# The norms' inverse root as Ln and Exp on ScalarE, in place of Sqrt there and a reciprocal on VectorE

## The chip, the cores and the metric

The kernel runs on one core of a Trainium2 chip. The metric is the time of one run on the device in microseconds, the median of three runs.

## The reference

Two transformer blocks over 512 tokens of 1024 columns, all in float32. The first block has a gated linear attention (GLA, 4 heads), a state-space layer (S5) and a mixture of 32 experts with 4 per token; the second has a state-space layer, a window attention, a full attention whose query and key heads are normed, and a gated ffn. Around and inside them stand RMS norms, all of one form:

```
def rmsnorm(x, g):
    xf = x.astype(jnp.float32)
    r = lax.rsqrt(jnp.mean(xf * xf, axis=-1, keepdims=True) + EPS)
    return (xf * r * g.astype(jnp.float32)).astype(x.dtype)

h = x
hn = rmsnorm(h, mix_pre_g) * (1 + sc1) + sh1        # first norm
...                                                 # GLA: o = rmsnorm(o, gla_norm_g) for each head; S5
h = h + g1 * rmsnorm(mix, mix_post_g)               # the mixer's post-norm
hn2 = rmsnorm(h, ffn_pre_g) * (1 + sc2) + sh2       # ahead of the router
h = h + g2 * rmsnorm(moe_ffn(hn2), ffn_post_g)      # the experts' post-norm
...                                                 # second block: norms of x and of the context,
...                                                 # of the q and k heads, ahead of the ffn, and the last one
```

## The kernel before

Activations are kept with the features on the 128 partitions and the tokens along the free dimension: a tensor of 1024 x 512 is 8 tiles of 128 x 512. A norm over features is therefore a sum over partitions. ScalarE squares each tile (line 415), TensorE multiplies the squares by a matrix of ones, so that each partition of one PSUM bank gets the sums of all 512 tokens (`pe_norm`), ScalarE takes the square root out of that bank (line 418), VectorE takes the reciprocal in place (line 437) and scales the 8 tiles by gain and inverse root (line 440), and ScalarE adds the shifts (line 424). Matmuls of the next layer wait for the last shifted tile.

There are 18 such norms, 16 over 512 columns and two over 256 (the context's). Their reciprocals stand in five places of VectorE's program: `dve_norm` (line 437, 5 of them), `dve_gla_out` (line 832, one for each of 4 heads), `dve_add_normed` (line 1284, the two post-norms with the addition to the residual), `dve_att_in` (line 2940, 5 heads' tiles of 512 columns and one of 256, in the second attention) and `dve_out` (line 3344). In the two loops over heads the steps share one buffer for the root. In GLA the head's outputs come from 22 matmuls, ScalarE squares and copies them (lines 867 and 869) once VectorE is done with the head before, and TensorE sums. In the second attention ScalarE squares the next head's tile (line 2916) right after the root of this one, and takes the next root when VectorE has scaled this head (line 2943). One more norm, of the state-space layer, has 4 columns with the tokens on the partitions; it keeps Sqrt and reciprocal.

Each engine runs its own program in order, and semaphores join them. `act_done` and `dve_done` are counted by an engine for itself: it waits on its own results before it reads them. ScalarE evaluates a function from the set of tables that is loaded. Where an activation needs a function outside the loaded set, the build puts a set load (ACT_TABLE_LOAD) in front of it. Copy, Square, Identity and Abs are in every set; Sqrt, Sin, Silu, Sigmoid, Gelu and Exp are each in others; one set has both Ln and Exp.

Weights come through six panel buffers (four in the second block) of 2 MB that the SP queue fills as TensorE gives them back. GpSimd loads the router's weights and biases after the mixer's post-norm (`pool_moe_loads`), and casts and subtracts the gate biases when they have landed (`pool_bias`, lines 1404 and 1408); that runs beside the norm ahead of the router.

Of the kernel before, what the change touches and what calls it, by code (L numbers as in the profile page):

```python
# [11 lines left out]
ACT = mybir.ActivationFunctionType  # L12
# [10 lines left out]
GLA_HEADS, DK, DV, CHUNK = 4, 64, 128, 64  # L23
# [12 lines left out]
HD = 64  # L36
# [243 lines left out]
def build(nc, a, table, where, out):  # L280

    ctx = ExitStack()
    with ctx:
# [23 lines left out]
        eps_col = sb("eps_col", [P, 1])  # L307
# [52 lines left out]
        act_done = sem("act_done")  # L360
# [41 lines left out]

        def act_norm(act, step, src, sq, std, n, kt, dim, shifts=None, dst=None, after=None, copied=False):

            for k in range(kt):
                if after is not None:
                    act.wait_ge(after.sem, after.next(act))
                if copied:  # L410
                    act.wait_ge(to_act.full, to_act.next_full())
                    bank = to_act.take()
                    act.activation(src[:, k, :], bank[:, 0:n], ACT.Copy).then_inc(to_act.free, 1)
                    act.wait_ge(to_act.free, to_act.own_reads())
                act.activation(sq[:, k, :], src[:, k, :], ACT.Square).then_inc(sq_ready.sem, 1)  # L415
            act.wait_ge(to_act.full, to_act.next_full())
            bank = to_act.take()
            act.activation(std, bank[:, 0:n], ACT.Sqrt, scale=1.0 / dim, bias=eps_col[:, 0:1]).then_inc(to_act.free, 1)
            act.wait_ge(to_act.free, to_act.own_reads())
            act.sem_inc(std_ready.sem, 1)  # L420
            if shifts is not None:
                for k in range(kt):
                    act.wait_ge(scaled.sem, scaled.next(act))
                    act.activation(dst[:, k, :], dst[:, k, :], ACT.Identity, bias=shifts[k]).then_inc(normed.sem, 1)  # L424
# [9 lines left out]

        def dve_norm(dve, step, src, dst, std, kt, factors):
            dve.wait_ge(std_ready.sem, std_ready.next(dve))
            dve.reciprocal(std, std).then_inc(dve_done, 1)
            dve.wait_ge(dve_done, step.next())
            for k in range(kt):
                dve.scalar_tensor_tensor(dst[:, k, :], src[:, k, :], factors[:, k:k + 1], std,  # L440
                                         ALU.mult, ALU.mult).then_inc(scaled.sem, 1)
# [242 lines left out]
        o_std = alr  # L684
# [144 lines left out]

        def dve_gla_out(dve, step, h):  # L830
            dve.wait_ge(ostd_ready.sem, ostd_ready.next(dve))
            dve.reciprocal(o_std, o_std).then_inc(dve_done, 1)
            dve.wait_ge(dve_done, step.next())
            dve.scalar_tensor_tensor(o_sb, o_sb, col("gla_norm_g"), o_std, ALU.mult, ALU.mult).then_inc(dve_done, 1)
            dve.wait_ge(dve_done, step.next())
            if h == 0:
                dve.wait_ge(gla_act.sem, gla_act.next(dve))
            dve.tensor_tensor(hidden[:, h, :], o_sb, og[:, h, :], ALU.mult).then_inc(dve_done, 1)
            dve.wait_ge(dve_done, step.next())
            dve.sem_inc(gla_out.sem, 1)  # L840

        def act_gla(act, step):
            act_project(act, step)
            act.wait_ge(gla_dve.sem, gla_dve.next(act))
            act.activation(work, bsum, ACT.Abs).then_inc(act_done, 1)
# [12 lines left out]
            act.activation(work, work, ACT.Exp, scale=1.0 / TAU).then_inc(act_done, 1)  # L858
            act.wait_ge(act_done, step.next())
            act.sem_inc(gla_act.sem, 1)  # L860
            act_project_rest(act, step)
            for h in range(GLA_HEADS):
                act.wait_ge(to_act.full, to_act.next_full())
                bank = to_act.take()
                if h >= 1:
                    act.wait_ge(gla_out.sem, gla_out.next(act))
                act.activation(o_sq, bank[:, :], ACT.Square).then_inc(act_done, 1)
                act.wait_ge(act_done, step.next())
                act.activation(o_sb, bank[:, :], ACT.Copy).then_inc(to_act.free, 1)
                act.wait_ge(to_act.free, to_act.own_reads())  # L870
                act.sem_inc(osq_ready.sem, 1)
                act.sem_inc(o_ready.sem, 1)
                act.wait_ge(to_act.full, to_act.next_full())
                bank = to_act.take()
                act.activation(o_std, bank[:, :], ACT.Sqrt, scale=1.0 / DV, bias=eps_col[:, 0:1]).then_inc(to_act.free, 1)
                act.wait_ge(to_act.free, to_act.own_reads())
                act.sem_inc(ostd_ready.sem, 1)


# [401 lines left out]
        def dve_add_normed(dve, step, branch, std, gains):  # L1281

            dve.wait_ge(std_ready.sem, std_ready.next(dve))
            dve.reciprocal(std, std).then_inc(dve_done, 1)
            dve.wait_ge(dve_done, step.next())
            for k in range(DT + 1):
                if k < DT:
                    dve.scalar_tensor_tensor(branch[:, k, :], branch[:, k, :], gains[:, k:k + 1], std,
                                             ALU.mult, ALU.mult).then_inc(dve_done, 1)
                if k:  # L1290
                    dve.wait_ge(dve_done, step.next())
                    dve.tensor_tensor(resid[:, k - 1, :], resid[:, k - 1, :], branch[:, k - 1, :], ALU.add)\
                        .then_inc(resid_tile.sem, 1)
            dve.wait_ge(resid_tile.sem, resid_tile.next(dve, DT))
            dve.sem_inc(resid_ready.sem, 1)
# [1605 lines left out]
        HEADS_NORMED = [(q_t[:, m, :], T) for m in range(4)] + [(k_t, T), (kc_t, CTX)]  # L2901

        def act_att_in(act, step, kind):
            if kind == 1:
                act.wait_ge(att_done.sem, att_done.next(act))
            for dst, n in (*[(q_t[:, m, :], T) for m in range(4)], (k_t, T), (kc_t, CTX),
# [7 lines left out]
            if kind == 1:  # L2914
                for i, (v, n) in enumerate(HEADS_NORMED):
# [4 lines left out]
                    bank = to_act.take()  # L2920
                    if i:
                        act.wait_ge(head_norm.sem, head_norm.next(act))
                    act.activation(nrm_std[:, 0:n], bank[:, 0:n], ACT.Sqrt, scale=1.0 / HD, bias=eps_col[:, 0:1]).then_inc(to_act.free, 1)
                    act.wait_ge(to_act.free, to_act.own_reads())
                    act.sem_inc(head_std.sem, 1)
            for dst, n in ((k_sw, T), (kc_sw, CTX)):
                act.wait_ge(to_act.full, to_act.next_full())
# [5 lines left out]
        def dve_att_in(dve, step, kind):  # L2933
# [3 lines left out]
            if kind == 1:  # L2937
                for i, (v, n) in enumerate(HEADS_NORMED):
                    dve.wait_ge(head_std.sem, head_std.next(dve))
                    dve.reciprocal(nrm_std[:, 0:n], nrm_std[:, 0:n]).then_inc(dve_done, 1)  # L2940
                    dve.wait_ge(dve_done, step.next())
                    gain = qk_gain[:, 0:1] if i < 4 else qk_gain[:, 1:2]
                    dve.scalar_tensor_tensor(v, v, gain, nrm_std[:, 0:n], ALU.mult, ALU.mult).then_inc(dve_done, 1)
                    dve.wait_ge(dve_done, step.next())
# [396 lines left out]

        def dve_out(dve, step):
            dve.wait_ge(std_ready.sem, std_ready.next(dve))
            dve.reciprocal(o_std2, o_std2).then_inc(dve_done, 1)
            dve.wait_ge(dve_done, step.next())
# [67 lines left out]
        def _(act):  # L3413
# [5 lines left out]
            act_silus(act, step)  # L3419
            act_s5_angles(act, step)  # L3420
            act_first_mods(act)
            act.wait_ge(resid_ready.sem, resid_ready.next(act))
# [4 lines left out]
            act_s5(act, step)  # L3427
            act_norm(act, step, mix, m_sq, m_std, T, DT, D, copied=True)
# [4 lines left out]
            act_extra(act, step)  # L3433
            act.wait_ge(turn, EXTRAS * STAGES + 1)
            act_norm(act, step, hidden[:, :, :], m_sq, m_std, T, DT, D)
            act_second_norms(act, step)
# [6 lines left out]
            act_merge(act, step)  # L3443
            act_ffn(act, step)
            act_out(act, step)

        @block.vector
# [53 lines left out]
```

## Time and profile before

| | us |
|---|---|
| median of 3 runs | 3699.09 |
| lowest and highest | 3698.45, 3699.99 |
| span of the profiled execution | 3697.6 |
| TensorE busy in it | 3222.1 |
| VectorE busy in it | 1277.0 |
| ScalarE busy in it | 486.5 |
| GpSimd busy in it | 264.7 |

The profiled execution has no run time of its own; its span, from the first to the last instruction, lies 1.5 us under the median. PE is TensorE, PEld its weight loads, DVE VectorE, ACT ScalarE, POOL GpSimd. Times in a row are microseconds from the start of the span, mean durations of a group nanoseconds. An entry such as "[9.38 <-ACTq L420]" says how long the engine had been idle and what ended that.

### The profile page before, as it was taken

The numbers are of one execution on the slowest core, as the hardware profiler recorded it, in microseconds if no ns is written. First come the engines' busy times: TensorE is split into PE (matmuls) and PEld (weight loads), VectorE is DVE, ScalarE is ACT, GpSimd is POOL, SyncE is SP. The second block draws the span as 40 slices with busy tenths as digits, with TensorE's granted clock in tenths as the row PEclk, the third lists the DMA queues.
The fourth block names the chain that finished last, engine by engine and source line by source line (L and its number), as shares of the span: only waits on it lengthen the run. The fifth ranks groups of instructions, "written<-read, shape, count | busy, mean of one in ns | idle before, by whom it ended". The sixth has DMA issues, their size and how long they took to land.

```text
span 3697.6 us, 33767 instructions
## 1 busy us (share of the span) xinstructions
PE 3222.1 (87%) x13683; PEld 1566.0 (42%) x13684; DVE 1277.0 (35%) x2091; ACT 486.5 (13%) x853; POOL 264.7 (7%) x352
## 2 busy tenths in 40 slices
PE   4894758799999999999994988987868999899998
PEld 2352223444443333433332646545646444344444
DVE  3126990523233323232333248605244011212201
ACT  1211001201000010001002210112224000100000
POOL 0005550200000000000000002100000000000000
PEclk8896769699999999999996897896879999999999
DMA  9411410298989999999992110010000122122210
GB/s 294 174 68 54 163 54 23 87 347 320 339 308 355 351 362 350 358 351 361 351 352 82 46 34 1 23 51 1 15 32 1 57 91 86 51 76 72 74 63 23
DMA packets 287683, 582.45 MB, mean 158 GB/s; under 512 B 7953, under 2 KB 12492, under 8 KB 287500
## 3 DMA queue, kind: packets, MB, share of 16 engines
q1 hardware_dynamic: 281184, 561.20, 42.3%
q0 software_dynamic: 5072, 15.80, 1.9%
q10 hardware_dynamic: 1276, 3.29, 0.3%
q8 instruction: 111, 1.82, 0.2%
q14 instruction: 40, 0.33, 0.0%
HBM read 576.08 MB, written 4.19 MB: 157 GB/s over the span
## 4 chain that ended last, share of the span: by engine, by line
PE 75%; DVE 16%; ACT 3%; issue 2%; SPq 1%; POOL 1%; ACTq 1%; DMA 1%; DVEq 0%; POOLq 0%; PEldq 0%
PE psum_all L211 72%; DVE scratch L1197 4%; PE psum_all L219 3%; DVE hidden L2039 2%; SPq L188 1%; DVE scratch L1221 1%; DVE scratch L2646 1%; DVE scratch L3059 1%; DVE scratch L2677 1%; ACTq L566 1%; DVE scratch L1214 1%; ACT scratch L3121 1%; DMA panel<-in_ada_w 1%; DVE scratch L2674 1%; DVE scratch L2940 1%
## 5 line engine op out<-in xcount | busy, mean ns | idle before, releaser
L211 PE MATMUL psum_all<-panel,scratch 128*64 128x512 f32 (+3 forms) x5568 | 977.7, 507 | 1.4 <-ACTq L1814 0.8
L211 PE MATMUL psum_all<-hidden,panel 128*128 128x512 f32 (+1 forms) x1808 | 794.0, 601 | 31.1 <-ACT hidden L424 20.9
L211 PEld LDWEIGHTS psum_all<-hidden,panel 128*128 128x128 f32 (+1 forms) x1808 | 346.2, 192 | 470.1 <-issue 439.7
L211 PEld LDWEIGHTS psum_all<-panel,scratch 128*64 128x64 f32 (+2 forms) x5568 | 333.8, 131 | 472.7 <-issue 426.1
L211 PE MATMUL psum_all<-scratch 128*128 128x64 f32 (+7 forms) x1592 | 388.0, 439 | 145.1 <-DVEq L1235 82.1
L211 PEld LDWEIGHTS psum_all<-scratch 128*128 128x128 f32 (+1 forms) x1592 | 250.9, 240 | 255.3 <-issue 98.3
L2039 DVE TENSOR_TENSOR hidden<-hidden,psum_all 128x512 f32<-128x512 f32 x264 | 169.7, 684 | 290.9 <-PE psum_all L211 290.9
L211 PE MATMUL psum_all<-scratch,panel 128*128 128x512 f32 (+1 forms) x672 | 250.5, 531 | 2.0 <-DVE resid L3246 1.0
L219 PE MATMUL psum_all<-const,scratch 128*128 128x128 f32 (+4 forms) x953 | 150.6, 297 | 111.5 <-DMA scratch<-in_s_lambda_im 33.0
L219 PEld LDWEIGHTS psum_all<-const,scratch 128*128 128x128 f32 (+4 forms) x953 | 109.7, 155 | 211.4 <-issue 105.2
L211 PE MATMUL psum_all<-scratch,const 128*128 128x512 f32 (+5 forms) x308 | 120.2, 535 | 82.8 <-ACT scratch L415 32.3
L211 PEld LDWEIGHTS psum_all<-scratch,panel 128*128 128x128 f32 x672 | 127.5, 190 | 127.5 <-issue 119.6
L2029 DVE SCALAR_TENSOR_TENSOR y_low<-psum_all,scratch,y_high 128x512 fp32r<-128x512 f32 (+1 forms) x49 | 33.6, 686 | 271.5 <-ACT y_high L2001 271.5
L211 PE MATMUL psum_all<-panel,hidden 128*128 128x512 f32 (+2 forms) x384 | 113.4, 461 | 10.4 <-ACT hidden L424 10.4
L211 PE MATMUL psum_all<-tokens_r,y_high 64*128 64x512 f32 (+2 forms) x360 | 97.0, 496 | 28.2 <-DVE hidden L2039 26.6
L211 PEld LDWEIGHTS psum_all<-scratch,const 128*128 128x128 f32 x308 | 59.1, 235 | 135.0 <-issue 68.2
L211 PE MATMUL psum_all<-panel 128*128 128x512 f32 x256 | 110.5, 592 | 1.7 <-DVEq L3237 1.7
L1425 POOL DMA_INDIRECT scratch<-token_rows,scratch x33 | 30.7, 931 | 1115.7 <-DVEq L1771 1115.7
L1812 ACT ACTIVATE scratch<-psum_all 128x512 f32<-128x512 f32 (+1 forms) x49 | 26.7, 545 | 617.8 <-PE psum_all L219 617.8
L1197 DVE TENSOR_TENSOR scratch<-scratch 128x512 f32<-128x512 f32 x128 | 104.8, 840 | 4.6
L2019 DVE TENSOR_SCALAR scratch<-psum_all 128x512 f32<-128x512 f32 (+1 forms) x49 | 30.7, 626 | 218.6 <-PE psum_all L211 218.6
L2535 DVE TENSOR_SCALAR scratch<-psum_all,cols 128x512 f32<-128x512 f32 (+1 forms) x44 | 33.0, 750 | 193.1 <-PE psum_all L211 193.1
(317 smaller groups left out, 2327.7 us busy)
## 6 DMA issues: line engine op xcount, KB each, us to landing
panel<-in_exp_w_gu SPq DMA_DIRECT2D x132, 2048.0 KB, 11.8
panel<-in_exp_w_down SPq DMA_DIRECT2D x66, 2048.0 KB, 14.4
panel<-in_w_in SPq DMA_DIRECT2D x17, 2048.0 KB, 7.9
panel<-in_ada_w SPq DMA_DIRECT2D x12, 2048.0 KB, 20.4
panel<-in_w_mod SPq DMA_DIRECT2D x12, 2048.0 KB, 7.9
panel<-in_ffn_w_gate SPq DMA_DIRECT2D x5, 2048.0 KB, 7.7
panel<-in_ffn_w_up SPq DMA_DIRECT2D x5, 2048.0 KB, 7.9
panel<-in_w_out SPq DMA_DIRECT2D x4, 2048.0 KB, 7.8
```

The source lines that it names most:

```text
L188: sp.dma_start(dst, src.rearrange("(k p) c -> p k c", p=P)).then_inc(self.loaded[s], 16)
L211: ins = self.pe.matmul(out, lhsT, rhs, start=start, stop=stop)
L219: return self.pe.transpose(out, in_, ident)
L566: act.dma_start(rows[at:at + n, tile_no, :], flat(name).rearrange("(r c) -> r c", c=P))\
L1197: tt = lambda o, x, y, op: dve.tensor_tensor(o, x, y, op)
L1214: dve.tensor_tensor_scan(z_re, mag, w1, 0.0, ALU.mult, ALU.add).then_inc(dve_done, 1)
L1221: dve.tensor_tensor_scan(z_im, mag, w3, 0.0, ALU.mult, ALU.add).then_inc(dve_done, 1)
L2039: dve.tensor_tensor(hidden[:, m, :], hidden[:, m, :], moe_y(no)[:, :], ALU.add).then_inc(shares_free, 1)
L2646: tt = lambda o, x, y, op: dve.tensor_tensor(o, x, y, op)
L2674: dve.tensor_tensor(decay[g][:, 4 * i:4 * i + 4, :], over(head_cols(acs, d, c, g)[:, 4 * i:4 * i + 4], P), bank[:, :].rearrange("p (h i) - ...
L2677: dve.tensor_scalar(decay[g], decay[g], 0.0, None, ALU.max).then_inc(dve_done, 1)
L2940: dve.reciprocal(nrm_std[:, 0:n], nrm_std[:, 0:n]).then_inc(dve_done, 1)
```

## The change

Ln takes the place of Sqrt, with the same scale and bias, and an Exp with scale -0.5 follows in place on ScalarE. The reciprocals of the 18 norms go. Seven `preload_act_table_set` calls load the set with both functions ahead of the places where it is used. The norm of 4 columns (line 2769) is not changed.

```
+        LN_EXP = "natural_log_exp_and_others"
+        def act_inverse_root(act, step, dst, sums, dim):
+            act.activation(dst, sums, ACT.Ln, scale=1.0 / dim, bias=eps_col[:, 0:1]).then_inc(to_act.free, 1)
+            act.wait_ge(to_act.free, to_act.own_reads())
+            act.activation(dst, dst, ACT.Exp, scale=-0.5).then_inc(act_done, 1)
+            act.wait_ge(act_done, step.next())
...
         def act_norm(act, step, src, sq, std, n, kt, dim, shifts=None, dst=None, after=None, copied=False):
...
-            act.activation(std, bank[:, 0:n], ACT.Sqrt, scale=1.0 / dim, bias=eps_col[:, 0:1]).then_inc(to_act.free, 1)
-            act.wait_ge(to_act.free, to_act.own_reads())
+            act_inverse_root(act, step, std, bank[:, 0:n], dim)
             act.sem_inc(std_ready.sem, 1)
...
         def dve_norm(dve, step, src, dst, std, kt, factors):
             dve.wait_ge(std_ready.sem, std_ready.next(dve))
-            dve.reciprocal(std, std).then_inc(dve_done, 1)
-            dve.wait_ge(dve_done, step.next())
...
         def act_gla(act, step):
...
             act_project_rest(act, step)
+            act.preload_act_table_set(LN_EXP)
             for h in range(GLA_HEADS):
...
-                act.activation(o_std, bank[:, :], ACT.Sqrt, scale=1.0 / DV, bias=eps_col[:, 0:1]).then_inc(to_act.free, 1)
-                act.wait_ge(to_act.free, to_act.own_reads())
+                act_inverse_root(act, step, o_std, bank[:, :], DV)
...
         def act_att_in(act, step, kind):
+            if kind == 0:
+                act.preload_act_table_set(LN_EXP)
...
-                    act.activation(nrm_std[:, 0:n], bank[:, 0:n], ACT.Sqrt, scale=1.0 / HD, bias=eps_col[:, 0:1]).then_inc(to_act.free, 1)
-                    act.wait_ge(to_act.free, to_act.own_reads())
+                    act_inverse_root(act, step, nrm_std[:, 0:n], bank[:, 0:n], HD)
...
             act_first_mods(act)
+            act.preload_act_table_set(LN_EXP)
             act.wait_ge(resid_ready.sem, resid_ready.next(act))
             act_norm(act, step, resid[:, :, :], n_sq, n_std, T, DT, D,
                      [mods[:, k, :] for k in range(DT)], hidden)
             act_gla(act, step)
             act_s5_setup(act, step)
             act_s5(act, step)
+            act.preload_act_table_set(LN_EXP)
             act_norm(act, step, mix, m_sq, m_std, T, DT, D, copied=True)
...
             act_extra(act, step)
+            act.preload_act_table_set(LN_EXP)
             act.wait_ge(turn, EXTRAS * STAGES + 1)
             act_norm(act, step, hidden[:, :, :], m_sq, m_std, T, DT, D)
...
             act_merge(act, step)
+            act.preload_act_table_set(LN_EXP)
             act_ffn(act, step)
+            act.preload_act_table_set(LN_EXP)
             act_out(act, step)
```

The reciprocals in `dve_gla_out`, `dve_add_normed`, `dve_att_in` and `dve_out` go in the same way as the one in `dve_norm`.

## Rows read from the trace of the kernel before

**Rows 1.** The page, busy time and share of each engine.
```profile
PE 3222.1 (87%) x13683; PEld 1566.0 (42%) x13684; DVE 1277.0 (35%) x2091; ACT 486.5 (13%) x853; POOL 264.7 (7%) x352
```

**Rows 2.** The chain that ended last, in order of time: start, length, what.
```profile
115.45 3.37 DVE scratch L437
...
162.12 84.57 PE psum_all L211 x196
...
2035.63 64.74 PE psum_all L211 x224
...
3677.39 3.36 DVE scratch L3344
```

**Rows 3.** Groups by line and shape: busy us, mean ns, idle before.
```profile
L3291 ACT ACTIVATE scratch<-scratch 128x512 f32<-128x512 f32 x22 | 13.8, 629 | 278.7 <-DVEq L2543 278.7
...
L437 DVE RECIPROCAL scratch<-scratch 128x512 f32<-128x512 f32 x4 | 13.4, 3353 | 30.7 <-ACTq L420 30.7
...
L418 ACT ACTIVATE scratch<-psum_all,eps_col 128x512 f32<-128x512 f32 x7 | 4.8, 687 | 31.3 <-PE psum_all L211 31.3
```

**Rows 4.** In order of time, first norm: start, length, engine, line, idle before.
```profile
105.02 4.26 ACT L415 ACTIVATE scratch<-resid 128x512 f32<-128x512 f32 x8
...
115.45 3.35 DVE L437 RECIPROCAL scratch<-scratch 128x512 f32<-128x512 f32 x1 [9.38 <-ACTq L420]
118.84 5.39 DVE L440 SCALAR_TENSOR_TENSOR hidden<-resid,small,scratch 128x512 f32<-128x512 f32 x8
```

**Rows 5.** In order of time, ScalarE in the gated attention.
```profile
166.04 1.28 ACT L847 ACT_TABLE_LOAD   x1
...
167.34 1.06 ACT L847 ACTIVATE scratch<-scratch 128x1024 f32<-128x1024 f32 x1
...
169.71 1.06 ACT L849 ACTIVATE scratch<-scratch 128x1024 f32<-128x1024 f32 x1
```

**Rows 6.** In order of time, the gated attention's heads.
```profile
271.26 3.59 PE L211 MATMUL psum_all<-scratch 128*128 128x128 f32 x22
...
277.30 0.60 ACT L867 ACTIVATE scratch<-psum_all 128x512 f32<-128x512 f32 x1 [5.10 <-DVEq L840]
...
278.62 2.08 PE L211 MATMUL psum_all<-scratch,const 128*128 128x512 f32 x2 [3.76 <-ACTq L871]
...
280.49 4.04 PE L211 MATMUL psum_all<-scratch 128*128 128x128 f32 x22
...
286.52 0.60 ACT L867 ACTIVATE scratch<-psum_all 128x512 f32<-128x512 f32 x1 [5.10 <-DVEq L840]
...
289.71 5.09 PE L211 MATMUL psum_all<-scratch 128*128 128x128 f32 x22
```

**Rows 7.** In order of time, the norm ahead of the router.
```profile
661.39 10.34 DVE L440 SCALAR_TENSOR_TENSOR hidden<-resid,small,scratch 128x512 f32<-128x512 f32 x8
...
664.41 1.28 POOL L1404 CAST bias_rows<-scratch 128x1024 fp32r<-128x1024 f32 x1 [2.54 <-DMA scratch<-in_exp_b_gu]
665.77 5.41 POOL L1408 TENSOR_TENSOR bias_rows<-scratch,bias_rows 32x1024 fp32r<-32x1024 f32 x2
```

**Rows 8.** In order of time, head norms of the second attention.
```profile
2697.20 1.12 PE L211 MATMUL psum_all<-scratch,const 128*128 128x512 f32 x2 [1.38 <-ACTq L2913]
...
2708.58 0.69 ACT L2923 ACTIVATE scratch<-psum_all,eps_col 128x512 f32<-128x512 f32 x1 [3.35 <-DVEq L2945]
...
2713.64 0.69 ACT L2923 ACTIVATE scratch<-psum_all,eps_col 128x512 f32<-128x512 f32 x1 [3.63 <-DVEq L2945]
...
2724.32 1.75 DVE L2940 RECIPROCAL scratch<-scratch 128x256 f32<-128x256 f32 x1 [0.71 <-ACTq L2925]
```

**Rows 9.** Windows: length, busy time of each engine, granted clock, DMA.
```profile
270.00:300.00 30.00, 19.80 (x74) 14.11 (x72) 15.83 (x12) 7.10 (x11) 0.00 (x0) 0.61 0.00 1
...
1110.00:1890.00 780.00, 760.84 (x5239) 299.94 (x5239) 245.61 (x445) 71.61 (x129) 34.88 (x103) 1.00 0.99 355
2699.00:2727.00 28.00, 9.82 (x11) 2.80 (x12) 22.76 (x12) 6.23 (x11) 0.00 (x0) 0.52 0.19 72
```

More of the change, by code:

```diff
@@ L399, in build, with act_inverse_root @@
         s5_out = signal("s5_out")
+        LN_EXP = "natural_log_exp_and_others"
+        def act_inverse_root(act, step, dst, sums, dim):
+            act.activation(dst, sums, ACT.Ln, scale=1.0 / dim, bias=eps_col[:, 0:1]).then_inc(to_act.free, 1)
+            act.wait_ge(to_act.free, to_act.own_reads())
+            act.activation(dst, dst, ACT.Exp, scale=-0.5).then_inc(act_done, 1)
+            act.wait_ge(act_done, step.next())
         def act_norm(act, step, src, sq, std, n, kt, dim, shifts=None, dst=None, after=None, copied=False):
@@ L417, in act_norm @@
             bank = to_act.take()
-            act.activation(std, bank[:, 0:n], ACT.Sqrt, scale=1.0 / dim, bias=eps_col[:, 0:1]).then_inc(to_act.free, 1)
-            act.wait_ge(to_act.free, to_act.own_reads())
+            act_inverse_root(act, step, std, bank[:, 0:n], dim)
             act.sem_inc(std_ready.sem, 1)
@@ L436, in dve_norm @@
             dve.wait_ge(std_ready.sem, std_ready.next(dve))
-            dve.reciprocal(std, std).then_inc(dve_done, 1)
-            dve.wait_ge(dve_done, step.next())
             for k in range(kt):
@@ L831, in dve_gla_out @@
             dve.wait_ge(ostd_ready.sem, ostd_ready.next(dve))
-            dve.reciprocal(o_std, o_std).then_inc(dve_done, 1)
-            dve.wait_ge(dve_done, step.next())
             dve.scalar_tensor_tensor(o_sb, o_sb, col("gla_norm_g"), o_std, ALU.mult, ALU.mult).then_inc(dve_done, 1)
@@ L861, in act_gla @@
             act_project_rest(act, step)
+            act.preload_act_table_set(LN_EXP)
             for h in range(GLA_HEADS):
@@ L874, in act_gla @@
                 bank = to_act.take()
-                act.activation(o_std, bank[:, :], ACT.Sqrt, scale=1.0 / DV, bias=eps_col[:, 0:1]).then_inc(to_act.free, 1)
-                act.wait_ge(to_act.free, to_act.own_reads())
+                act_inverse_root(act, step, o_std, bank[:, :], DV)
                 act.sem_inc(ostd_ready.sem, 1)
@@ L1283, in dve_add_normed @@
             dve.wait_ge(std_ready.sem, std_ready.next(dve))
-            dve.reciprocal(std, std).then_inc(dve_done, 1)
-            dve.wait_ge(dve_done, step.next())
             for k in range(DT + 1):
@@ L2903, in act_att_in @@
         def act_att_in(act, step, kind):
+            if kind == 0:
+                act.preload_act_table_set(LN_EXP)
             if kind == 1:
@@ L2922, in act_att_in @@
                         act.wait_ge(head_norm.sem, head_norm.next(act))
-                    act.activation(nrm_std[:, 0:n], bank[:, 0:n], ACT.Sqrt, scale=1.0 / HD, bias=eps_col[:, 0:1]).then_inc(to_act.free, 1)
-                    act.wait_ge(to_act.free, to_act.own_reads())
+                    act_inverse_root(act, step, nrm_std[:, 0:n], bank[:, 0:n], HD)
                     act.sem_inc(head_std.sem, 1)
@@ L2939, in dve_att_in @@
                     dve.wait_ge(head_std.sem, head_std.next(dve))
-                    dve.reciprocal(nrm_std[:, 0:n], nrm_std[:, 0:n]).then_inc(dve_done, 1)
-                    dve.wait_ge(dve_done, step.next())
                     gain = qk_gain[:, 0:1] if i < 4 else qk_gain[:, 1:2]
@@ L3343, in dve_out @@
             dve.wait_ge(std_ready.sem, std_ready.next(dve))
-            dve.reciprocal(o_std2, o_std2).then_inc(dve_done, 1)
-            dve.wait_ge(dve_done, step.next())
             for k in range(DT):
@@ L3421, in _ @@
             act_first_mods(act)
+            act.preload_act_table_set(LN_EXP)
             act.wait_ge(resid_ready.sem, resid_ready.next(act))
@@ L3427, in _ @@
             act_s5(act, step)
+            act.preload_act_table_set(LN_EXP)
             act_norm(act, step, mix, m_sq, m_std, T, DT, D, copied=True)
@@ L3433, in _ @@
             act_extra(act, step)
+            act.preload_act_table_set(LN_EXP)
             act.wait_ge(turn, EXTRAS * STAGES + 1)
@@ L3443, in _ @@
             act_merge(act, step)
+            act.preload_act_table_set(LN_EXP)
             act_ffn(act, step)
+            act.preload_act_table_set(LN_EXP)
             act_out(act, step)
```

## The prediction

> **What bounds the kernel now.** I read the busy shares first [rows 1]: TensorE is busy for 87% of the span, so the span is TensorE's work plus the places where it stands still. The chain that ended last then shows where it stands still: between long stretches of matmuls [rows 2] stand single reciprocals on VectorE and the steps next to them. The reader is to see that fifteen of its stretches are a 512-column reciprocal of 3.36 us each, the first at 115 and the last at 3677 us, with TensorE waiting behind it. The list of groups by shape gives the prices [rows 3], and the order in time around each norm says what else ends just behind the reciprocal [rows 4, 6 to 8]. That last reading decides the sum: a reciprocal that goes is worth its length only until the next thing is late.
>
> **The exchange in one norm.** Removed: a reciprocal of 3.353 us [rows 3]; from its start to the start of the first scaling are 118.84 - 115.45 = 3.39 us [rows 4]. Sqrt becomes Ln with the same operands (PSUM in, a bias column, scale), 0.687 us [rows 3]; Exp and Ln in the trace both take 1.06 us on the same 1024 columns, so the function does not set the price [rows 5]. Added: an Exp in place, SBUF to SBUF, no bias column. The nearest row is Silu of that form and shape, 0.629 us [rows 3]; with 0.03 us for the wait on its own result it is 0.66. The row of the other form (bias column, PSUM) bounds it at 0.72 and the 0.60 copies of the heads' loop [rows 6] from below. So T = 3.39 - 0.66 = 2.73 us for 512 columns (2.67 to 2.79). For 256 columns: 1.75 + 0.04 [rows 8] less an Exp that I estimate at 0.42 (0.629 less 256 columns, at the 0.83 ns a column by which 1024 columns cost 1.06 and 512 cost 0.629) and 0.03: 1.34 us. VectorE loses 18 instructions, which nobody else waited for.
>
> **Five plain norms.** The mixer's post-norm (reciprocal at 641 us), the experts' post-norm (1985), the second block's first norm (2026), its ffn norm (3202) and the final norm (3677) have the pattern of rows 4: sums, root, reciprocal, eight scalings, and TensorE waits for the whole chain. The set load in front of each lies under the sums of squares before and after. 5 x 2.73 = 13.65. The context's norm (256 columns, 2009) is a link of the same chain: 1.34.
>
> **The first norm.** Same pattern, 2.73, but its preload is queued on ScalarE just ahead of the eight squares that start at 105.02 [rows 4], with no wait left to hide it; squares, sums and root all follow it. Before, the load came behind the squares. A load costs 167.34 - 166.04 = 1.30 us of ScalarE from start to next start [rows 5]. Net 2.73 - 1.30 = 1.43. The other six preloads stand where ScalarE waits for TensorE or for its turn: nothing, and 1.30 each if that cover went.
> The Trainium skill, page "ScalarE: Activation LUTs", section "What ACT_TABLE_LOAD costs", puts a switch at about 2.66 us, since it adds a drain of about 1.38 to the 1.28 of the load itself. The rows show the 1.28 but the next activation 0.02 us behind it, so I take the trace; by the page the first norm would give 0.07 instead of 1.43.
>
> **Loads that go away.** In the gated attention Exp, Ln, Exp load three sets [rows 5], in dt four more, and one stands before each attention's first Exp and the router's. All serve activations under long TensorE stretches or before activations that wait for VectorE: 162.12 to 246.69 and 2035.63 to 2100.37 are matmuls without a stop [rows 2]. Worth nothing; 1.30 each at most where this is wrong.
>
> **The four heads' norms** [rows 6]. A head takes 286.52 - 277.30 = 9.22 us: two 0.60 activations, the sum (2.08), the root, the reciprocal and two VectorE operations. Less T that is 6.49. But the next head's output matmuls (x22) start only after the sum and then take 3.59, 4.04 and 5.09 us in the three cases. Head 1: the chain would be back at 277.30 - 2.73 = 274.57, the matmuls end at 271.26 + 3.59 = 274.85; gain 2.4. Head 2: the sum starts 278.62 - 277.30 = 1.32 after that, at 276.2, the matmuls 280.49 - 278.62 = 1.87 later at 278.1 and end at 282.1; before it was 286.52: gain 4.4 so far. Head 3: sum 283.5, matmuls 285.3 to 290.4; before 9.22 after 286.52, 295.74: 5.3 so far. The last one has nothing behind it: 2.7. Together 8.0 instead of 4 x 2.73 = 10.9. With every group at 5.09 it is 7.0; with all at 1.2 GHz gone it is 10.9. I take 8.0.
>
> **The norm before the router** [rows 7]. T again, and more. VectorE's eight scalings take 10.34 us here and 5.39 in rows 4, because GpSimd's bias cast and subtractions begin at 664.41 and hold VectorE up. They start when bias transfers have landed that were issued after the post-norm, so not sooner for this norm's sake. With Exp the scalings start at 661.39 - 2.73 = 658.66 and end at 664.05, 0.36 us before the cast. So 2.73 + 4.95 = 7.68. Below: the cast comes a little sooner in that run and stalls the last scalings, 2.73. I take 7.7, since what GpSimd then delays (small VectorE tables, needed only after 14 us of router matmuls) is not late.
>
> **The six head norms of the second attention** [rows 8]. They are serial: roots at 2708.58 and 2713.64, 5.06 apart. By VectorE alone a step would take 5.06 - 3.39 + 0.66 = 2.3 us. But the square of the next head is queued on ScalarE behind Exp, and its sum (the pair of matmuls that takes 2.08 in rows 6) must end before the next Ln. That loop is Ln 0.72 + Exp 0.66 + square 0.63 with two signals that I estimate at 0.1 each + sum 2.08 = 4.3. So a step gains 0.8, not 2.7: four steps 3.1, the step to the 256-column head (its square and sum are shorter, 3.2 in all) 1.8, the end 1.3. Together 6.3. With the sum at 1.12, as the first one ran [rows 8], 4.3 more: 10.6.
>
> **Sum.** 13.65 + 1.34 + 1.43 + 8.0 + 7.7 + 6.3 = 38.4 us. Everything between is shifted as a whole: in the experts TensorE is busy for 761 of 780 us at full clock [rows 9] and its panels are asked for as it frees them, so the stage neither gives back nor adds. The profiled execution has a span of 3697.6 and the median run 3699.09, 1.5 above, which stays: 3699.1 - 38.4 = 3660.7.
>
> **The rivals.**
> A. *The clock stays up.* Between 270 and 300 the mean granted clock is 0.61, in the six head norms 0.52 [rows 9], that is, mostly the 1.2 GHz level. TensorE rests less in both loops then. If it stays at 2.4 GHz in them, GLA gives 10.9 and the head norms 10.6: 7.2 more, 3653.5. Against it: the groups in GLA's loop grow from 3.59 to 5.09 us head by head [rows 6], so the clock was on its way down there, and the sums of the head norms take the long 2.08. The Trainium skill, "TensorE: Matmul & The Clock Gate", Part 1, says that recent activity releases the gate; the rows agree on two levels, and by it less rest can only help.
> B. *GpSimd still meets the scalings*: 4.95 less, 3665.7. For it: the margin is 0.36 us, and half of them may meet it. With 7.0 for GLA too, 3666.7.
> C. *Every reciprocal counts in full*, with nothing behind it: 16 x 2.73 + 2 x 1.34 = 46.4, less the preload 45.1, with the router's 4.95 50.0: 3649. Against it are the two loops above, where something stands less than T behind.
> D. *The preloads do not hold, and each function gets the set that its own search finds*, as Exp, Ln, Exp do now [rows 5]: two loads a norm, 36 x 1.30 = 46.8, 8.4 slower than before: 3707.5. It turns slower only from 38.4 / 1.30 = 30 exposed loads on. Against it: ScalarE waits for sums before nearly every Ln, so 18 of them are covered, which leaves 23.4 and 3684; and one set holds both, so nothing asks for another load.
> The Trainium skill's "ScalarE: Activation LUTs", in "Table sets: the hidden batching unit", says the same of that set.
>
> **Chances.** Forecast as worked out 0.63; A in whole or part 0.15; B 0.14; C beside A 0.03; D 0.03 with covered loads and 0.01 with all exposed; 0.01 for no change at all. The measurement tells 0.2%, 7.4 us, from no change; only D's end and the last are not faster. Faster 0.97, same 0.01, slower 0.02. The range goes from A (3653.5) to B (3667), with 2 us on both sides for where the clock rises after the ten gaps that get shorter: 3651 to 3669.
>
> **What would show it.** Right: no reciprocal of 512 columns; pairs of activations of 0.69 and 0.63 us with 0.03 between; a load of 1.28 us between the last small copy and the first square at 105 us; the router's scalings in 5.4 us; about 4.3 us from Ln to Ln in the six head norms, each released by TensorE. Wrong: loads between Ln and Exp, scalings still at 10 us, a step of 3.3 or of 5, or another length of the experts' stage than before; the last would move the time more than any term here.

## The result, and the profile after it

The changed kernel ran in a median of 3654.53 us (four runs, 3648.19 to 3660.16) against 3699.35 us (3698.45 to 3699.99) of the kernel before: a ratio of 0.9879, 95% interval 0.9864 to 0.9894. It is faster, and the interval is clear of 1; 3660.7 was forecast. Six more executions of it, in experiment 1, lay between 3654.09 and 3663.80; all ten have a mean of 3658.6. The profiled one took 3660.16 us with a span of 3658.1, so 39.5 us of span went away, against 38.4 in the sum.

The page after, the busy row and two groups by line and shape (busy us, mean ns, idle before):

```profile
PE 3212.4 (88%) x13683; PEld 1561.3 (43%) x13684; DVE 1215.4 (33%) x2073; ACT 485.4 (13%) x862; POOL 264.3 (7%) x352
```
```profile
L409 ACT ACTIVATE scratch<-psum_all,eps_col 128x512 f32<-128x512 f32 x16 | 11.0, 687 | 55.5 <-PE psum_all L211 55.5
L411 ACT ACTIVATE scratch<-scratch 128x512 f32<-128x512 f32 x16 | 10.1, 629 | 0.5
```

VectorE lost 18 instructions [rows 1]; Ln (L409) costs what the root cost, 687 ns, and Exp (L411) 629 ns, both as taken from [rows 3]. The 0.5 us of idle time before 16 Exps says that nothing, no load either, stands between the two.

**The first norm**, in order of time (to be read beside [rows 4]):

```profile
102.25 1.28 ACT L3421 ACT_TABLE_LOAD   x1
...
103.54 4.26 ACT L424 ACTIVATE scratch<-resid 128x512 f32<-128x512 f32 x8
104.31 9.82 PE L211 MATMUL psum_all<-scratch,const 128*128 128x512 f32 x16 [2.38 <-ACT scratch L424]
114.17 0.69 ACT L409 ACTIVATE scratch<-psum_all,eps_col 128x512 f32<-128x512 f32 x1 [6.36 <-PE psum_all L211]
114.89 0.63 ACT L411 ACTIVATE scratch<-scratch 128x512 f32<-128x512 f32 x1
115.69 5.39 DVE L446 SCALAR_TENSOR_TENSOR hidden<-resid,small,scratch 128x512 f32<-128x512 f32 x8 [12.38 <-ACTq L428]
```

From the start of Ln to the first scaling are 115.69 - 114.17 = 1.52 us, where 4.23 stood: T, the gain of the exchange in one norm, was 2.71. The load delays the squares by 1.29. What the sum did not have is the 9.82 us of the sixteen sum matmuls; before, 8.77:

```profile
105.80 8.77 PE L211 MATMUL psum_all<-scratch,const 128*128 128x512 f32 x16 [1.11 <-ACT scratch L415]
```

**The gated heads** (to be read beside [rows 6]):

```profile
265.10 0.60 ACT L872 ACTIVATE scratch<-psum_all 128x512 f32<-128x512 f32 x1 [19.37 <-PE psum_all L211]
...
266.43 2.08 PE L211 MATMUL psum_all<-scratch,const 128*128 128x512 f32 x2 [1.36 <-ACTq L876]
...
268.29 3.63 PE L211 MATMUL psum_all<-scratch 128*128 128x128 f32 x22
...
271.96 0.60 ACT L872 ACTIVATE scratch<-psum_all 128x512 f32<-128x512 f32 x1 [2.08 <-PE psum_all L211]
...
273.29 1.79 PE L211 MATMUL psum_all<-scratch,const 128*128 128x512 f32 x2 [1.36 <-ACTq L876]
...
274.87 3.76 PE L211 MATMUL psum_all<-scratch 128*128 128x128 f32 x22
...
278.66 0.60 ACT L872 ACTIVATE scratch<-psum_all 128x512 f32<-128x512 f32 x1 [2.20 <-PE psum_all L211]
...
281.43 3.88 PE L211 MATMUL psum_all<-scratch 128*128 128x128 f32 x22
...
291.74 1.76 DVE L1054 MEMSET scratch<- 128x2048 f32 x1 [0.60 <-DVE hidden L842]
```

The two ends of the same loop before:

```profile
268.07 0.60 ACT L867 ACTIVATE scratch<-psum_all 128x512 f32<-128x512 f32 x1 [20.75 <-PE psum_all L211]
...
305.41 1.76 DVE L1050 MEMSET scratch<- 128x2048 f32 x1 [0.60 <-DVE hidden L838]
```

The square of a head is now released by TensorE and no longer by VectorE: the output matmuls behind the sum end last, as the prediction had it. But the groups took 3.63, 3.76 and 3.88 us instead of growing to 5.09, and the sums fell from 2.08 us head by head to 1.52. A head takes 6.7 to 6.9 us, and the loop is 10.7 us shorter (37.34 to 26.64, from the first square to VectorE's first work behind it), not 8.0.

**The norm before the router** (to be read beside [rows 7]):

```profile
642.72 5.39 DVE L446 SCALAR_TENSOR_TENSOR hidden<-resid,small,scratch 128x512 f32<-128x512 f32 x8 [3.56 <-ACTq L428]
...
648.45 1.24 POOL L1406 CAST bias_rows<-scratch 128x1024 fp32r<-128x1024 f32 x1 [2.50 <-DMA scratch<-in_exp_b_gu]
648.97 1.25 PE L211 MATMUL psum_all<-scratch,hidden 128*128 128x32 f32 x5 [7.71 <-issue]
```

The scalings take 5.39 us and are over at 648.11, 0.34 us before the cast (0.36 was forecast). From the start of the scalings to the start of the router's matmuls are 648.97 - 642.72 = 6.25 us; before they were 672.59 - 661.39 = 11.20 [rows 7, and the row below]. The difference is 4.95 us, the second part of that term of the sum.

```profile
672.59 3.81 PE L211 MATMUL psum_all<-scratch,hidden 128*128 128x32 f32 x17 [15.39 <-issue]
```

**The six head norms** (to be read beside [rows 8]):

```profile
2662.72 0.63 ACT L2920 ACTIVATE scratch<-scratch 128x512 f32<-128x512 f32 x1
...
2669.03 0.69 ACT L409 ACTIVATE scratch<-psum_all,eps_col 128x512 f32<-128x512 f32 x1 [2.21 <-PE psum_all L211]
2669.75 0.63 ACT L411 ACTIVATE scratch<-scratch 128x512 f32<-128x512 f32 x1
2670.46 0.75 DVE L2944 SCALAR_TENSOR_TENSOR scratch<-scratch,qk_gain 128x512 f32<-128x512 f32 x1 [3.47 <-ACTq L2928]
2670.50 0.63 ACT L2920 ACTIVATE scratch<-scratch 128x512 f32<-128x512 f32 x1
...
2671.23 2.07 PE L211 MATMUL psum_all<-scratch,const 128*128 128x512 f32 x2 [2.23 <-ACTq L2922]
2673.34 0.69 ACT L409 ACTIVATE scratch<-psum_all,eps_col 128x512 f32<-128x512 f32 x1 [2.21 <-PE psum_all L211]
...
2707.68 0.90 ACT L3122 ACTIVATE scratch<-psum_all,scratch 128x768 f32<-128x768 f32 x1 [4.47 <-DVEq L3069]
```

Ln to Ln is 4.31 us, and the ring is in the rows: Ln, Exp, square, sum, next Ln, each Ln released by TensorE. VectorE's scaling at 2670.46 releases nothing that is late. From the first square to the attention's first Exp the stage takes 2707.68 - 2662.72 = 44.96 us; before, it was 2747.60 - 2696.36 = 51.24:

```profile
2696.36 0.63 ACT L2916 ACTIVATE scratch<-scratch 128x512 f32<-128x512 f32 x1
...
2747.60 0.90 ACT L3121 ACTIVATE scratch<-psum_all,scratch 128x768 f32<-128x768 f32 x1 [3.03 <-DVEq L3068]
```

**Windows** (length; busy time of PE, PEld, DVE, ACT and POOL; granted clock, share and GB/s of DMA): the heads' loop, the head norms, the experts, and the second attention, which no term of the sum spoke of.

```profile
265.00:291.00 26.00, 17.75 (x75) 12.57 (x74) 7.02 (x10) 10.04 (x16) 0.00 (x0) 0.70 0.00 1
2663.00:2687.00 24.00, 10.85 (x13) 3.02 (x14) 4.24 (x6) 10.76 (x18) 0.00 (x0) 0.57 0.25 88
1085.00:1865.00 780.00, 760.84 (x5233) 300.05 (x5235) 247.06 (x447) 71.45 (x128) 35.01 (x103) 1.00 0.99 355
...
2707.70:2835.80 128.10, 109.72 (x729) 86.68 (x730) 55.91 (x102) 51.13 (x102) 0.00 (x0) 0.91 0.00 1
```

The same stretch before:

```profile
2747.60:2869.30 121.70, 103.40 (x729) 82.25 (x730) 55.89 (x102) 51.07 (x101) 0.00 (x0) 0.96 0.00 1
```

The same 729 matmuls were busy for 6.3 us more at a mean clock of 0.91 instead of 0.96. So in this execution the second attention took back all that the head norms in front of it gave. Was that the change, or the execution?

### The profile page after: what moved, and what is told of

Same layout as the page of the kernel before. It is cut to its first block, busy times and chain, and to the rows that moved or that the text cites. A ratio compares the mean times of both kernels' runs of the same rounds, so it can differ in the third digit from the quotient of the medians.

```text
span 3658.1 us, 33758 instructions
## 1 busy us (share of the span) xinstructions
PE 3212.4 (88%) x13683; PEld 1561.3 (43%) x13684; DVE 1215.4 (33%) x2073; ACT 485.4 (13%) x862; POOL 264.3 (7%) x352
## 4 chain that ended last, share of the span: by engine, by line
PE 76%; DVE 15%; ACT 3%; issue 2%; SPq 1%; POOL 1%; DMA 1%; ACTq 1%; DVEq 0%; POOLq 0%; PEldq 0%
PE psum_all L211 73%; DVE scratch L1201 4%; PE psum_all L219 3%; DVE hidden L2041 2%; SPq L188 1%; DVE scratch L2648 1%; DVE scratch L1225 1%; DVE scratch L3060 1%; DVE scratch L2679 1%; ACTq L572 1%; DVE scratch L1218 1%; ACT scratch L3122 1%; DMA panel<-in_ada_w 1%; DVE scratch L2676 1%; ACT hidden L432 0%
## 5 line engine op out<-in xcount | busy, mean ns | idle before, releaser
L211 PE MATMUL psum_all<-tokens_r,y_high 64*128 64x512 f32 (+2 forms) x360 | 96.7, 494 | 28.2 <-DVE hidden L2041 26.6
```

The costliest lines, as they stand in the source:

```text
L211: ins = self.pe.matmul(out, lhsT, rhs, start=start, stop=stop)
```

## The experiments

All times of a stage below are differences of the same two starts in each profile.

**1. The changed kernel again, and twice more.** No edit: four more executions, one of them with a profile, and later two single executions, each with a profile.

> The changed kernel once more, unaltered, in five rounds. Its first four runs lay at 3648.2, 3649.0, 3660.1 and 3660.2 us, and the profiled one (3660.2) has twelve stretches of the second attention as before but two groups of 20 matmuls at 5.37 us in place of 2.83. Theory 1 (TensorE's clock falls in some runs at the block ends of that attention and adds about 3 us each time): the runs again fall into clusters, and a profiled run near 3648 has no 5.37 groups or fewer of them, while one near 3660 has two or more. Theory 2 (the two clusters come from the start, where the first loads and the first norm lie 2.8 us earlier or later): all groups of 20 have the same lengths in both clusters and the first square's start differs by about 11 us. The median is expected at 3649 to 3660, 39 to 51 us under the kernel before.

> The changed kernel unedited, one more profile. Its executions so far lay between 3648 and 3664 us, those of the kernel before between 3696 and 3704; both profiled ones were at 3660 and 3664. Theory: a short execution differs from these only in the start (up to 5 us until the first square, 103.5 and 107.2 us so far) and in the second attention (121.8 to 128.1), all other stages within 0.3 us; at 3650 it would have a start under 103.5 and an attention of 122. Rival: another stage carries the difference.

> The same kernel and the same expectation once more, on the same chip.

Measured: 3663.65 us (3662.8 to 3663.8; ratio 0.9903, interval 0.9886 to 0.9919), then 3654.09 and 3660.75. The second attention, the row of each of the last two kernels' profiles:

```profile
2707.80:2829.80 122.00, 103.56 (x729) 82.39 (x730) 55.88 (x102) 51.16 (x102) 0.00 (x0) 0.96 0.00 1
```
```profile
2705.60:2835.50 129.90, 111.30 (x729) 87.16 (x730) 55.85 (x102) 51.12 (x102) 0.00 (x0) 0.90 0.00 1
```

One kernel, unedited: 128.1, 126.9, 122.0 and 129.9 us in four executions, with the same 729 matmuls and a granted clock of 0.91, 0.92, 0.96 and 0.90. So the stage's time differs from execution to execution. The starts of the first square lay at 103.5, 107.2, 106.9 and 107.1 us, less than 4 apart where the second theory of the first repeat asked for some 11; no execution near 3648 has a profile, so what made the two shortest ones is not shown. The expectation that only the start and the second attention move was too narrow: the first attention up to the head norms took 184.2, 184.3, 180.2 and 177.5 us (185.3 before), and the stretch between the gated heads and the first Gelu 91.3, 91.2, 93.1 and 93.1. The loop of the gated heads was steady at 26.64, 26.61, 26.87 and 26.90 us, and the head norms at 44.9 to 45.0.

**2. The first load earlier.**

```diff
-            act_first_mods(act)
             act.preload_act_table_set(LN_EXP)
+            act_first_mods(act)
```

> The changed kernel with the first set load moved ahead of the first modulation rows, where ScalarE waits for TensorE. Theory 1 (the load costs its 1.30 us on the path in front of the first square and nothing else): first square 0.1 to 0.2 us after the last small copy instead of 1.57, time 1.3 us less than the changed kernel, and the same sums of squares. Theory 2 (the late start also made the first sums slower, 9.82 us for 16 matmuls against 8.77 before): 2.3 us less from the last small copy to the root. Theory 3 (a load drains the engine for 1.4 us more than its row shows): 2.7 us less.

Measured: 3660.34 us (3654.79 to 3664.08), ratio 0.9891, interval 0.9875 to 0.9908. The rows of its first norm:

```profile
104.30 4.27 ACT L424 ACTIVATE scratch<-resid 128x512 f32<-128x512 f32 x8
...
105.08 8.80 PE L211 MATMUL psum_all<-scratch,const 128*128 128x512 f32 x16 [1.10 <-ACT scratch L424]
```

TensorE waits 1.10 us ahead of the sums instead of 2.38, and the sums take 8.80 instead of 9.82: against the profile above the load's old place cost 1.29 + 1.02 = 2.3 us and not 1.30, as the second theory had it. Over all fourteen profiles of this case the sums took 8.65 to 8.80 in the seven without a load ahead of the squares, and 8.52, 8.66, 9.79, 9.82, 10.08, 10.09 and 10.14 in the seven with it: longer in five of seven, and not in the two single executions. So the longer sums often come with the load, not always. On the whole time 2.3 us are inside the spread of either kernel's runs.

**3. No preloads.** All seven calls of `preload_act_table_set` out, nothing else.

> The changed kernel without its seven preloads, so that the build places the loads by itself. Theory 1 (the build takes one set for Ln and another for Exp, a load costs 1.30 us, and the one in front of Ln lies under the wait for the sums): two loads a norm, each Exp starts about 1.30 later after its Ln. The plain norms lose 1.30 each (8 of them 10.4, less the first preload's 1.3), GLA's four heads 1.3 each where VectorE's chain is then the longer (at most 5.2, since the output matmuls have 0.1 to 1 us behind it), the six head norms 1.3 each 7.8: 18 to 22 us slower than the changed kernel, 3670 to 3678, still faster than before. Theory 2 (a load costs 2.66 with its drain): 42 to 48 slower, at or above the time before. Theory 3 (the build keeps the common set once it is loaded): one load a stage, within 3 us of the changed kernel.

Measured: 3684.42 us (3679.53 to 3688.04), ratio 0.9955, interval 0.9939 to 0.9972. ScalarE in its head norms:

```profile
2702.12 1.28 ACT L409 ACT_TABLE_LOAD   x1 [0.22 <-DVEq L2943]
2704.11 0.69 ACT L409 ACTIVATE scratch<-psum_all,eps_col 128x512 f32<-128x512 f32 x1 [0.70 <-PE psum_all L211]
2704.81 1.28 ACT L411 ACT_TABLE_LOAD   x1
2706.11 0.63 ACT L411 ACTIVATE scratch<-scratch 128x512 f32<-128x512 f32 x1
```

Without the preload Ln and Exp each get a set of their own: 36 loads of 1.28. The Ln's load lies under the sum (Ln then still waits 0.70 for TensorE), the Exp's is open: from Ln to Exp 2.00 us instead of 0.72. This is the prediction's rival D in its covered form, and its 3684 and the median of 3684.42 agree; that they do so within half a microsecond is luck, since the four runs spread over 8.5 us and the difference to the preloaded kernel was 20.8 us on the same chip, not 23.4. The rows also give the price of a load: from the start of the load to the start of the Exp are 1.30 us. The Trainium skill, "ScalarE: Activation LUTs", section "What ACT_TABLE_LOAD costs", puts a switch at about 2.66; the rows here differ, and by them it is half of that.

**4. The clash with GpSimd alone.** The kernel before, with GpSimd's bias work held until the router norm is done:

```diff
             pool_moe_loads(pool)
+            pool.wait_ge(normed.sem, normed.next(pool, 2 * DT))
             pool_bias(pool, step)
```

> The kernel BEFORE (Sqrt and reciprocals), with GpSimd's bias cast and subtractions held back until the norm ahead of the router is done. Theory 1 (these three GpSimd operations held up the eight scalings, 10.34 us instead of 5.39): the scalings take 5.4 us, the router's matmuls start 5.0 us earlier relative to the reciprocal, and the time is 5.0 us less than before, 3694.4. Theory 2 (the scalings are slow there for another reason, such as the bias transfers): 10.3 us still and no change. Theory 3 (the work only moves and holds up VectorE in the router): scalings 5.4, but the 3 to 5 us come back between the router's matmuls and the first expert.

Measured: 3690.63 us (3689.31 to 3694.81, ten runs), ratio 0.9979, interval 0.9969 to 0.9988.

```profile
662.52 5.39 DVE L440 SCALAR_TENSOR_TENSOR hidden<-resid,small,scratch 128x512 f32<-128x512 f32 x8
663.31 5.36 ACT L424 ACTIVATE hidden<-hidden,mods 128x512 f32<-128x512 f32 x8 [4.25 <-DVE hidden L440]
668.73 1.05 POOL L1404 CAST bias_rows<-scratch 128x1024 fp32r<-128x1024 f32 x1 [6.17 <-ACT hidden L424]
```

With the reciprocal still there, but no cast beside them, the scalings take 5.39 us. From the first scaling to VectorE's first read of the router's logits are 20.2 us in place of 25.2, and from there to its selection of the first expert's tokens 40.7 in both profiles. So 5.0 us were GpSimd's, and nothing of its delayed work is late. The median fell by 8.0 us, 3 more than that; the interval, 4.4 to 11.5 us, holds 5.0, and this profile, of an execution of 3694.81 us, does not show the rest.

**5. Two buffers for the head norms' squares.** On the changed kernel:

```diff
-        nrm_sq, nrm_std = part(7424, T), part(8192, T)
+        nrm_sqs, nrm_std = (part(7424, T), part(8960, T)), part(8192, T)
...
+                act_head_square(0)
                 for i, (v, n) in enumerate(HEADS_NORMED):
+                    if i + 1 < len(HEADS_NORMED):
+                        act_head_square(i + 1)
                     act.wait_ge(to_act.full, to_act.next_full())
```

> The changed kernel, with two buffers for the squares of the second attention's six head norms: the square of head i+1 is taken before the Ln of head i, so its sum on TensorE lies under Ln, Exp and scaling. Theory (the loop Ln, Exp, square, sum sets the step of 4.30 us): now Ln 0.72, Exp 0.66 and the scaling with its signals (about 0.9) set it, 2.3 us; from the first head's square to the attention's first exponential 45.0 becomes 36 to 37 us, and the kernel is about 8.5 us faster than the changed one. Rival (VectorE or the waits between the engines set the step): the step stays over 4 and the stage at 45. Third: the step falls to 3.3, because square, Ln and Exp and a sum at the slower clock still share it.

Measured: 3652.06 us (3649.63 to 3654.44), ratio 0.9869, interval 0.9854 to 0.9884. From the first square to the attention's first Exp 36.42 us instead of 44.96. The median lies 6.5 us under the mean of the changed kernel.

```profile
2673.51 0.69 ACT L409 ACTIVATE scratch<-psum_all,eps_col 128x512 f32<-128x512 f32 x1 [0.24 <-DVEq L2951]
...
2675.85 0.69 ACT L409 ACTIVATE scratch<-psum_all,eps_col 128x512 f32<-128x512 f32 x1 [0.24 <-DVEq L2951]
```

A step is 2.34 us and released by VectorE. The 8.5 us were TensorE's sum standing in the ring, as the theory had it.

**6. The same edit in the kernel before**, a control.

> The same edit in the kernel before the change, as a control. Theory: there the step of 5.06 us is root, reciprocal and scaling, and the sum ends earlier, so nothing happens: 51.2 us from the first square to the first exponential, step 5.06, within 0.1% of the kernel before. Rival (the sum sets part of the step there too): the stage falls by 2 us or more.

Measured: 3700.84 us (3697.81 to 3704.74, ten runs) against 3700.54, ratio 1.0002, interval 0.9992 to 1.0011; the stage 50.9 us (51.2). The sum was free as long as the reciprocal stood beside it.

**7. Two buffers in the gated heads.** On the changed kernel, TensorE issues the output matmuls of head h+1 ahead of the sum of head h, and the squares and masks go one head earlier to suit:

```diff
+                if h:
+                    pe_gla_sum(h - 1)
+            pe_gla_sum(GLA_HEADS - 1)
```

> The changed kernel, with two buffers each for the output and its square of the four gated heads: TensorE issues the output matmuls of head h+1 ahead of the sum of head h, ScalarE squares head h+1 ahead of the Ln of head h, VectorE masks the scores of head h+2 ahead of scaling head h. Theory (since the reciprocal went, the sum and then the next head's output matmuls behind it set the loop): the period falls from 6.6 to 6.9 us to a matmul group and a sum, 3.8 + 1.6 = 5.4, and the time from the first head's square to the end of the loop falls from 26.4 to about 20.5, 6 us. Rival (Ln, Exp and the two VectorE steps set the loop): the period stays at 6.6 or over. Rival (the clock falls less as TensorE rests less): groups at 2.5 to 3, the loop at 17 or 18.

Measured: 3655.05 us (3648.87 to 3663.92), ratio 0.9881, interval 0.9865 to 0.9898; the total cannot tell it from the changed kernel. The loop itself takes 22.88 us instead of 26.64, 3.8 less and not 6.

```profile
271.71 2.07 PE L211 MATMUL psum_all<-scratch,const 128*128 128x512 f32 x2
...
273.57 3.51 PE L211 MATMUL psum_all<-scratch 128*128 128x128 f32 x22
...
277.98 2.76 PE L211 MATMUL psum_all<-scratch 128*128 128x128 f32 x22
...
281.60 0.60 ACT L877 ACTIVATE scratch<-psum_all 128x512 f32<-128x512 f32 x1 [1.71 <-DVEq L849]
```

The matmuls left the ring, which shows that they had set it. Some of the gain is the clock's: the last three sums took 1.12 us each, where the changed kernel had 1.79 to 1.52. But the first sum now stands behind a second group (5.07 us after the first square in place of 1.33), and the last heads wait for VectorE. I had counted the steps in the middle, and the start of the loop too short by 2 us: the group ahead of that first sum took 5.25 us.

**8. All three together**: 2, 5 and 7.

> The changed kernel with the first preload moved ahead of the last small copies, the two square buffers of the head norms and those of the gated heads. If the three add up: 2.5 + 8.5 + 6 = 17 us below the changed kernel, about 3641, give or take the 7 us by which the second attention and the start differ from run to run; 3636 to 3650. If the clock gives something back after the shorter gaps, less than 12 us.

Measured: 3640.59 us (3639.37 to 3646.05), ratio 0.9846, interval 0.9832 to 0.9859: 1.5% below the kernel before, and 18 below the mean of the changed one. In its profile the first norm gives 2.3 us (first square to shift 11.9 with no load ahead), the heads' loop 4.0 and the head norms 9.9.

**9 and 10. The head norms alone, both ways.** The changed kernel with root and reciprocal back in the six head norms, and the kernel before with Ln and Exp only there.

> The changed kernel with the six head norms of the second attention put back to root and reciprocal. Sure part: from the first square to the first exponential 51.2 us again in place of 45.0. The question is the attention behind it, which took 121.7 to 122.0 us in all three profiles with the reciprocal there and 123.8 to 128.1 in all seven without it, in groups of matmuls that ran at the lower clock some 75 and 103 us after the first exponential. Theory (the shorter head norms bring these stretches): 122 us again, so the undone kernel ends within 2 us of the changed one. Rival (they come with where the run stands against a beat of the clock's control, whatever the norm): 124 to 128 us here too, and the kernel is 6 us slower than the changed one.

> The kernel before with the six head norms alone changed to Ln and Exp, their set loaded ahead of the second attention's projections. 51.2 becomes 45.0 from the first square to the first exponential. By the theory the attention behind it grows from 121.8 to 124 to 128 us, and 0 to 4 us of the 6.3 are left; by the rival it stays at 122 here about as often as not, and all 6.3 are left.

Measured: 3663.63 us (3655.57 to 3666.67), ratio 0.9899, interval 0.9882 to 0.9916; and 3694.94 us (3691.83 to 3701.63, ten runs), ratio 0.9994, interval 0.9984 to 1.0004. The head norms take 51.2 us when undone; changed alone, 43.6 (the 1.4 us under 45.0 lie behind the last Exp; up to there both take 23.0). The second attention took 126.1 us with the reciprocal back and 125.3 in the other. So my theory that the shorter head norms bring the long attention falls, by one profile: it was long with the reciprocal too. The medians move as they should, 5 us above the mean of the changed kernel and 4 below the kernel before, but the second interval includes 1.0: in the whole time one term of 6.2 us is not told apart from the spread of the attention behind it.

## Why the prediction was right, and where it was off

1. **The exchange.** T was 2.73 and measured 2.71 to 2.73; the stages of the ffn norm and the final norm shrank by 2.7 each, and that of the mixer's post-norm and the router's norm by 5.4. Right.
2. **The first norm**: 1.43 forecast, 2.72 - 1.29 - 1.05 = 0.38 measured. The 1.05 of longer sums was missing. TensorE stood still 1.27 us longer ahead of them (2.38 for 1.11), and in five of seven profiles with the load there the sums were longer, in two they were not (experiment 2). The context's norm lost to longer sums too, 6.55 instead of 5.47 us, which left 0.3 of its 1.34; no load was added there, and in one of the four executions of the changed kernel these sums took 5.2.
3. **The gated heads**: mechanism right (TensorE releases each square, experiment 7 takes it out), size wrong: 10.7 for 8.0. The mis-sized term is the matmul group, taken at 3.59, 4.04 and 5.09 from the rows of before; together they took 1.5 us less, and the four sums 1.3 less. The granted clock of the loop is 0.70, and it was 0.61 in [rows 9]: part of rival A, which came true in this loop alone. The prediction's lower value for it, 7.0 "with every group at 5.09", does not follow from its own chain: that gives 5.6, and 7.0 needs the first group at its 3.59. All seven profiles of the heads' loop with Ln and Exp, preloaded and otherwise unedited, had 26.6 to 26.9 us, and all four with the reciprocal 37.3.
4. **The router norm**: 7.7 forecast, 2.72 + 4.95 = 7.67 measured, the margin to the cast 0.34 us. Rival B did not happen, and experiment 4 shows that its price was right (5.0).
5. **The head norms**: 6.3 forecast, 6.2 measured, step 4.31 for 4.3. Rival A's 10.6 did not happen there: the clock was at 0.57, the 512-column sums took 2.07. Experiment 5 shows that another order takes TensorE out of the ring.
6. **Rival C** (every reciprocal in full) is out by point 5, 6.2 us where it had 5 x 2.73 + 1.34 = 15.0; in the gated heads it came close, 10.7 of 10.9. **Rival D** is out with the preloads; without them its loads and its cover are what experiment 3 shows.
7. **"The stage neither gives back nor adds"** was right for the experts' own work: 760.84 us of TensorE in 780 again, and 1177.7 us from the first sigmoid of their gates to the last in all fourteen profiles. From that last one to the root of the norm behind it, it was not: 66.4 to 67.0 us in the four profiles with the reciprocal there, 64.1 to 64.7 in eight of the ten others and 66.7 in two. The same work, before and after:

```profile
1917.80:1984.60 66.80, 41.32 (x149) 14.66 (x146) 14.75 (x23) 8.13 (x13) 0.00 (x0) 0.74 0.47 173
```

```profile
1894.40:1958.50 64.10, 38.68 (x150) 13.97 (x147) 14.74 (x23) 8.14 (x14) 0.00 (x0) 0.79 0.49 179
```

TensorE was busy for 2.6 us less at a granted clock of 0.79 for 0.74. Nor was it right for the rest, as the prediction used it. The first attention gave 1.1 in the profiled run and 7.8 in another; the second cost 6.4, 5.2, 0.2 and 8.1 in the four profiles. The terms as measured add to 5 x 2.72 + 0.3 + 0.4 + 10.7 + 7.7 + 6.2 = 38.9, against 39.5 of the whole span. That these two are so near is luck: the profiled execution was 2.8 us sooner at the first norm, gave 2.7 behind the experts and 1.1 in the first attention, and lost 6.4 in the second. The ten executions average 40.5 us less than 3699.1; they spread over 16 us, while those of the kernel before spread over 8. The range of the prediction gave these stretches 2 us on either side, too little for a single execution: two of the ten, 3648.19 and 3649.01, lie under its 3651.

What stays open: why the same matmuls get the lower clock in one execution of the second attention and not in the next. Time of arrival alone doesn't decide it by the profiles here: with starts of the attention within 0.2 us at 2707.7 and 2707.8 it took 128.1 and 122.0. Nor do the runs settle whether the change makes the long attention likelier. The kernel before and its edits of experiments 4 and 6 took 121.7, 121.7 and 122.0 us, and of the eleven profiles with Ln and Exp anywhere only one took 122.0; the others took 123.8 to 129.9, and the eleven average 125.8. If that is no chance, some 4 us there are a cost of the change that no term of the sum has.

## What to carry to other kernels

Price a removed wait by what becomes free right behind it, in the profile's order of time, instruction by instruction: that gave 6.3, with 6.2 measured, in a loop where the reciprocals in full come to 15.0, and it found 5 extra microseconds in a norm where a neighbour engine had been in the way. When two functions share a table set, load that set once by name ahead of them, and put the load where its engine already waits: left to itself each function took its own set, and the kernel was 21 us above the preloaded one on the same chip (3684.42 and 3663.65). Once the slow step is gone, look at the buffers that were free while it lasted; a second one was worth nothing before the change and 8.5 us of its stage after it.

## What the runs showed of the hardware

With a load of 1.28 us ahead of eight squares, the sixteen matmuls behind it took 9.8 to 10.1 us in five of seven profiles and 8.5 and 8.7 in two; without it they took 8.65 to 8.80 in all seven. Eight VectorE scalings of 512 columns took 10.34 us beside GpSimd's cast and subtractions and 5.39 without them. And one unedited kernel ran the same 729 matmuls of its second attention in 103.6 to 111.3 us of busy time, at a mean granted clock of 0.96 to 0.90.
